# A two-direction gated delta rule: 64-wide block matrices, and the next tile pair's preparation inside the recurrence

## What is computed

```python
CHUNK = 64
gc = cumsum(chunks(g))                                   # running decay in a chunk
decay = exp(where(lower, gc[..., :, None] - gc[..., None, :], -inf))   # 64 x 64
nil = where(strict, -einsum('nbhid,nbhjd->nbhij', kb, kc) * decay, 0)  # 64 x 64
tinv = eye(64) + nil; power = nil
for _ in range(5):
    power = power @ power
    tinv = tinv + tinv @ power
w_v  = tinv @ (vc * bc)
k_cd = tinv @ (kb * exp(gc))
# the recurrence, chunk after chunk
v_new = w_v - k_cd @ state
o     = (qc * exp(gc)) @ state + (qc kc^T * decay) @ v_new
state = state * exp(g_last) + k_dec^T @ v_new
```

## Time and profile before

| | |
|---|---|
| median of 3 executions | 3482.56 us (3478.14 to 3482.67) |
| the profiled execution | 3480.33 us |
| its span, first to last instruction | 3478.5 us |
| PE busy | 3211.5 us, 92% of the span |
| DVE, ACT, POOL busy | 1343.4, 1095.5, 1170.1 us |
| mean granted clock of PE | 0.969 |
| delta stage, layer 0 | 264.0 to 635.4 us |
| delta stage, layer 1 | 2194.1 to 2496.6 us |

### The profile page before, as it was taken

How to read it: one execution, slowest core, us unless ns; L and a number is a source line. 1 busy time by engine, 2 the same in 40 slices (tenths; PEclk the granted TensorE clock), 3 DMA queues, 4 the chain that set the end, 5 groups by cost and what they waited for, 6 DMA issues and landing times.

```text
span 3478.5 us, 49823 instructions
## 1 busy us (share of the span) xinstructions
PE 3211.5 (92%) x21019; PEld 2728.1 (78%) x21019; DVE 1343.4 (39%) x1765; ACT 1095.5 (31%) x1742; POOL 1170.1 (34%) x753
## 2 busy tenths in 40 slices
PE   5998999998889999799999989899999999989997
PEld 3887888876668888588888767789877778768885
DVE  4684434234561112422222368644424631232222
ACT  2442222223552212222222244432323542232222
POOL 4234333421203333323223232544531324444443
PEclk7999999999999999899999979999999999989999
DMA  5214433210002232122222121000111013423331
GB/s 196 67 33 155 158 111 104 67 53 20 9 6 64 64 100 67 34 65 61 67 61 61 55 73 43 25 1 1 49 55 31 10 51 99 136 62 97 97 93 59
DMA packets 303660, 231.41 MB, mean 67 GB/s; under 512 B 16784, under 2 KB 275280, under 8 KB 302544
## 3 DMA queue, kind: packets, MB, share of 16 engines
q1 hardware_dynamic: 297360, 204.55, 19.7%
q0 software_dynamic: 3776, 17.91, 1.4%
q10 hardware_dynamic: 2304, 5.77, 0.4%
HBM read 217.19 MB, written 11.98 MB: 66 GB/s over the span
## 4 chain that ended last, share of the span: by engine, by line
PE 82%; DVE 8%; issue 4%; ACT 3%; POOL 2%; DMA 0%; ACTq 0%; POOLq 0%; DVEq 0%
PE ps L409 19%; PE ps L410 19%; PE ps L411 19%; PE ps L653 3%; PE ps L668 3%; PE ps L494 2%; DVE stat L1188 2%; PE ps L515 1%; PE ps L713 1%; PE ps L700 1%; PE ps L532 1%; PE ps L421 1%; PE ps L717 1%; PE ps L701 1%; DVE R L1161 1%
## 5 line engine op out<-in xcount | busy, mean ns | idle before, releaser
L1536 POOL TENSOR_TENSOR wl<-wring,wh 128x1024 fp32r<-128x1024 f32 (+1 forms) x312 | 721.1, 2314 | 1368.2 <-ACT wh L922 1368.2
L409 PE MATMUL ps<-hh,wh 128*128 128x512 f32 (+1 forms) x2592 | 932.8, 360 | 90.1 <-DVE hl L1167 77.5
L410 PE MATMUL ps<-hl,wh 128*128 128x512 f32 (+1 forms) x2592 | 915.2, 353 | 0.0
L411 PE MATMUL ps<-hh,wl 128*128 128x512 f32 (+1 forms) x2592 | 914.4, 353 | 0.0
L409 PEld LDWEIGHTS ps<-hh,wh 128*128 128x128 f32 x2592 | 497.4, 192 | 179.1 <-issue 53.8
L410 PEld LDWEIGHTS ps<-hl,wh 128*128 128x128 f32 x2592 | 498.2, 192 | 67.8 <-issue 4.1
L411 PEld LDWEIGHTS ps<-hh,wl 128*128 128x128 f32 x2592 | 497.1, 192 | 66.3
L922 ACT ACTIVATE wh<-wring 128x1024 fp32r<-128x1024 f32 (+1 forms) x312 | 307.8, 988 | 523.6 <-PE ps L411 497.4
L1471 DVE SCALAR_TENSOR_TENSOR R<-ps,modcs,R 128x512 f32<-128x512 f32 x216 | 136.3, 659 | 387.7 <-PE ps L411 386.7
L410 PE MATMUL ps<-fl,wh 128*128 128x512 f32 (+1 forms) x768 | 274.8, 358 | 0.0
L411 PE MATMUL ps<-fh,wl 128*128 128x512 f32 (+1 forms) x768 | 274.5, 357 | 0.0
(11 more groups left out here) (232 smaller groups left out, 4791.2 us busy)
## 6 DMA issues: line engine op xcount, KB each, us to landing
wring<-in_w_ffn SPq DMA_DIRECT2D x128, 512.0 KB, 4.0
wring<-in_w_in SPq DMA_DIRECT2D x116, 512.0 KB, 3.8
wboth<-in_w_mod SPq DMA_DIRECT2D x80, 512.0 KB, 6.1
wring<-in_w_branch SPq DMA_DIRECT2D x48, 256.0 KB, 2.8
wring<-in_w_out SPq DMA_DIRECT2D x16, 512.0 KB, 3.8
x_store<-R POOLq DMA_DIRECT2D x2, 3072.0 KB, 9.6
R<-x_store POOLq DMA_DIRECT2D x2, 3072.0 KB, 11.6
R<-in_w_mod SPq DMA_DIRECT2D x7, 512.0 KB, 13.4
```

The source lines that it names most:

```text
L409: mm(ps[:, t0:t1], ahk, rh[:, k, t0:t1], start=(k == 0), stop=False)
L410: mm(ps[:, t0:t1], ahk, rl[:, k, t0:t1], start=False, stop=False)
L411: last = mm(ps[:, t0:t1], alk, rh[:, k, t0:t1], start=False, stop=(k == kn - 1))
L1536: G.tensor_tensor(slot_view(wl, n % NSPL, l, name, i), w, slot_view(wh, n % NSPL, l, name, i).bitcast(F32), ALU.subtract)\
```

## The change

The block-diagonal matrices are now kept as what they are: 64 wide, one chunk in partitions 0 to 63 and the other in 64 to 127 of a [128, 4, 64] buffer. Masks and identity are 64 wide too. Then:

- Every product of two such matrices is two products of 64 x 64 x 64 per head, one for each chunk, in alternation (`halves`): chunk 0 in rows and columns 0 to 63 of the array, chunk 1 in rows and columns 64 to 127. Key and query products (`key_products`) are 64 columns wide, chunk 0 and chunk 1 in alternation.
- The transpose of the next power is no longer a transpose of ACT's copy: it is a product of its own (the transposed power squared), issued with `pw` (`halves(ps[:, 512:768], src, srcT)`). AT is a product with the identity.
- ACT's, DVE's and POOL's operations on these matrices have 256 columns instead of 512.
- `vn` and the output products compute only the chunk's 64 rows, with the two directions (which are at different chunks, `chunk = (c, 1 - c)`) in alternation, head by head; `so` alternates the directions too, and both directions' `so` come before the outputs. DVE adds both states before it adds outputs, and PE's next `vn` waits for `read_first`, that is for the state alone; with output, `so` has a mark of its own (`pe_done "S"`) for it.
- The next pass's preparation moves into the recurrence of this one: `delta_decays` (bc, W, and the exponentials for the queries, which now have two buffers) after `vn` of the first chunk, `delta_keys` (G, A) after `vn` of the second, `delta_turned` (AT) after the second chunk's products. Only `Q` and X0 stay at the head of a pass. For pass 0 the three stand ahead of the loop, and no pass's R waits for `z_saved` now.
- kcd writes its two chunks to two banks; kbe and kd share a buffer (`kbuf`).

The diff, cut to its core (ACT's and DVE's lists follow the same pattern; POOL's order is shown further down):

```diff
+        qdbuf = [[r(U0 + 5120 * d + 512 * b, 2, 4, HALF) for d in range(2)] for b in range(2)]
+        kbuf, vnbuf, vbbuf = ([r(U0 + 5120 * d + at, 4, P) for d in range(2)] for at in (1024, 2048, 4608))
+        cdbuf = [r(U0 + 5120 * d + 1536, 2, 4, HALF) for d in range(2)]
+        rbuf, wbuf, pbuf, p2buf, tbuf, t2buf, xbuf, aqbuf = (
+            [r(U0 + 5120 * d + at, 4, HALF) for d in range(2)] for at in range(2560, 4608, 256))
...
+            def halves(out, left, right):
+                for h in range(C_H):
+                    for lo in (0, HALF):
+                        last = mm(out[lo:lo + HALF, h * HALF:h * HALF + HALF], left[lo:lo + HALF, h, :],
+                                  right[lo:lo + HALF, h, :], start=True, stop=True)
+                return last
+            def delta_decays(l, s, d):
+                pe.wait_ge(*pool_done.at("R", l, s, d))
+                ps = take(pe, "bc", l, s, d)
+                rows = [flat(rbuf[d])[lo:lo + HALF, :] for lo in (0, HALF)]
+                for c, lo in enumerate((0, HALF)):
+                    mm(ps[:, 512 * c:512 * c + 256], ones[lo:lo + HALF, :], rows[c], start=True, stop=True)
+                for c, lo in enumerate((0, HALF)):
+                    last = mm(ps[lo:lo + HALF, 256:512], ones[lo:lo + HALF, 0:HALF], rows[c], start=True, stop=True)
...
                         for d in range(2):
                             src, srcT, dst, dstT = power(d, i)
                             pe.wait_ge(*(read("pw", l, s, d, i - 1) if i else read("AT", l, s, d)))
                             ps = take(pe, "pw", l, s, d, i)
-                            for h in range(C_H):
-                                last = mm(ps[:, h * P:h * P + P], srcT[:, h, :], src[:, h, :], start=True, stop=True)
+                            last = halves(ps, srcT, src)
+                            if i < 4:
+                                last = halves(ps[:, 512:768], src, srcT)
                             last.then_inc(*filled("pw", l, s, d, i))
                         for d in range(2):
                             src, srcT, dst, dstT = power(d, i)
-                            if i < 4:
-                                pe.wait_ge(*read_first("pw", l, s, d, i))
-                                for h in range(C_H):
-                                    last = tr(pair("pw", l, s, d, i)[:, 512 + h * P:512 + h * P + P], dst[:, h, :], ident)
...
+                            pe.wait_ge(*read("pw", l, s, d, i))
                             pe.wait_ge(*(read("X", l, s, d, i - 1) if i else dve_done.at("X0", l, s, d)))
+                            halves(take(pe, "X", l, s, d, i), dst, xbuf[d]).then_inc(*filled("X", l, s, d, i))
...
+                        new = [take(pe, "vn", l, n, d) for d in range(2)]
+                        for h in range(C_H):
+                            o = [new[d][at[d]:at[d] + HALF, h * P:h * P + P] for d in range(2)]
+                            for d in range(2):
+                                mm(o[d], cdbuf[d][:, chunk[d], h, :], S[:, 4 * d + h, :], start=True, stop=False)
+                            for d in range(2):
+                                ins = mm(o[d], xbuf[d][at[d]:at[d] + HALF, h, :], vbbuf[d][at[d]:at[d] + HALF, h, :],
+                                         start=False, stop=True)
...
+                        if s + 1 < TT:
+                            for d in range(2):
+                                (delta_decays, delta_keys)[c](l, s + 1, d)
                         for d in range(2):
                             pe.wait_ge(*read("vn", l, n, d))
                             pe.wait_ge(*pool_done.at("kd", l, s, d))
...
+                    if s + 1 < TT:
+                        for d in range(2):
+                            delta_turned(l, s + 1, d)
```

DVE's list in a doubling step keeps its order, for each direction first the copy of the transposed power, then the addition of X:

```diff
                         for d in range(2):
                             if i < 4:
-                                dve.wait_ge(*pe_done.at("pwT", l, s, d, i))
-                                V.tensor_copy(flat(power(d, i)[3]), pair("pw", l, s, d, i)[:, 512:1024])\
+                                dve.wait_ge(*full("pw", l, s, d, i))
+                                V.tensor_copy(flat(power(d, i)[3]), pair("pw", l, s, d, i)[:, 512:768])\
                                     .then_inc(*free("pw", l, s, d, i, by=1))
                             dve.wait_ge(*full("X", l, s, d, i))
-                            V.tensor_tensor(flat(xbuf[d]), pair("X", l, s, d, i)[:, 0:512], flat(xbuf[d]), ALU.add)\
+                            V.tensor_tensor(flat(xbuf[d]), pair("X", l, s, d, i)[:, 0:256], flat(xbuf[d]), ALU.add)\
```

More of the change, by code:

```diff
@@ L222, in power @@
         def power(d, i):
-            one, two = (pbuf[d], tbuf[d]), (p2buf[d], rbuf[d])
+            one, two = (pbuf[d], tbuf[d]), (p2buf[d], t2buf[d])
             return (*one, *two) if i % 2 == 0 else (*two, *one)
@@ L1007, in _ @@
+                for d in range(2):
+                    delta_decays(l, 0, d)
+                for d in range(2):
+                    delta_turned(l, 0, d)
                 for s in range(TT):
                     for d in range(2):
-                        act.wait_ge(*full("bc", l, s, d))
-                        if s:
-                            act.wait_ge(*full("vn", l, 2 * s - 1, d))
-                        A(flat(ebuf[d]), pair("bc", l, s, d)[:, 0:512], ACT.Exp).then_inc(*free("bc", l, s, d, by=1))
@@ L1021, in _ @@
-                    for d in range(2):
-                        act.wait_ge(*full("AT", l, s, d))
-                        A(flat(tbuf[d]), pair("AT", l, s, d)[:, 0:512], ACT.Copy).then_inc(*free("AT", l, s, d))
+                        delta_queries(l, s, d)
                     for i in range(5):
@@ new lines, in _ @@
+                        for d in range(2):
+                            t, cc = tiles[d][s], (c if d == 0 else 1 - c)
+                            if out_wanted:
+                                lo = 64 * cc
+                                o, new = Otok[lo:lo + 64, t, :], pair("so", l, n, d)[lo:lo + 64, 512:1024]
+                                dve.wait_ge(*full("so", l, n, d))
+                                if (t, cc) in seen:
+                                    V.tensor_tensor(o, new, o, ALU.add).then_inc(*free("so", l, n, d, by=1))
+                                else:
+                                    V.tensor_copy(o, new).then_inc(*free("so", l, n, d, by=1))
+                                seen.add((t, cc))
```

336 lines of the change are left out of this document (188 added, 148 removed).

## The result

The changed kernel takes **3416.68 us** (median of 4 runs, 3411.79 to 3422.39), where the kernel before took 3482.61 (4 runs, 3478.14 to 3483.76) on the same chip: a ratio of 0.9817, with a 95% interval of 0.9805 to 0.9828. It is faster, by 66 us, and inside the range of the prediction. But the forecast was 132 us, and of these only half came. The profiled execution has a span of 3417.9 us at a mean granted clock of 0.952 (before: 3478.5 and 0.969).

A forecast was written before the change was run, and what follows sets the result against it. PE, busy 92% of the span, was taken to bound the kernel. Savings of 69.0 us in layer 0 and 63.0 in layer 1, 132 together off 3480.3, gave 3350 us; own range 3300 to 3385, stated range 3300 to 3430.

The forecast's parts named there:

- the clock falls: Rival: PE's waits in doubling steps drop the clock to the 1.2 GHz level; 3395 us, or 3438; chance 0.20.
- record of the 64 x 64 pair: PE's time per matmul record in alternating 64-wide products: 0.0275 us, bounds 0.0275 and 0.055.
- doubling step, wait in it: One doubling step takes 3.8 us instead of 4.46, with PE waiting 1.15 us for DVE's copy.
- kcd to `vn`: From kcd's start to `vn`: 32 records in 1.76 us, then ACT's copies, 2.65 us in all.
- change of tile shape: Each switch of PE between full-row and 64-row tiles costs 0.15 us, bounds 0 and 0.19.
- pass without, with output: Layer 1 passes: 36.2 us without output against 45.25 before, 40.5 with output against 52.4.
- last kcd to projection: In a layer's last pass, from kcd to the first projection: 19.65 us, including 1.5 us waits for `vn` copies.
- waits for modulation weights: SP's weight loads for layer 0's modulation blocks: costed at nothing, up to 10 us if their cover fails.
- earlier start, layer 0: At layer 0's start the chain W, A, AT, Q in half-size operations becomes 3.2 us shorter.
- The overlap of the two diagonal tiles: The two chunks' 64 x 64 tiles run side by side on PE; the no-overlap rival gave 3490 us, chance 0.12.
- DVE's T(1) behind add(0): In each doubling step DVE's second transposed copy follows its first addition, so PE waits 1.15 us before X(1).
- granted clock of 1.00: PE stays at the 2.4 GHz level in the delta stages' passes, as in the profile before; no loss summed.

The follow-up runs named there:

- e6: Changed kernel with e4's unread products, modulation blocks spread evenly over layer 0's doubling steps, and last-pass ACT query work after both `vn` copies: 3380.77 us.
- e1: Changed kernel with the 64 x 64 products reordered, all four heads of chunk 0 first, then all four of chunk 1: 3464.23 us.
- e2: Changed kernel with DVE copying both directions' transposed powers before it adds to either X: 3377.85 us.
- e3: Changed kernel with all full-row matmuls first, then all 64-row ones, in `vn` and outputs, `start` and `stop` only at first and last head: 3344.91 us.
- e4: Changed kernel with unread products put into PE's waits, in doubling steps, between kcd and `vn`, and ahead of some `so`: 3381.32 us.
- e9: Changed kernel with unread products only in the first four doubling steps of each pass, 48 in all: 3415.93 us.
- e10: Changed kernel with only one unread product in each pass, between kcd and `vn`, 12 in all: 3395.55 us.
- e5: Changed kernel with decays, key products and turned matrix back at the head of their own pass, products still 64 wide: 3490.04 us.

## Why the prediction was right or wrong

Right in sign and in range; the forecast itself missed half. The outcome lies where the rival "the clock falls" put it (3395, at most 3438; chance 0.20), but that is in part luck: the clock took 35 us, and another 34 that this rival didn't have came on top. And the range held because it had been drawn to take in the clock's case; its own range for the forecast ended at 3385.

| Term of the prediction | said | measured |
|---|---|---|
| record of the 64 x 64 pair | 0.0275 us | 0.0292 |
| doubling step, wait in it | 3.8, 1.15 | 3.94, 0.93 |
| kcd to `vn` | 2.65 | 3.0 to 3.1 |
| change of tile shape | 0.15 | 0.15 |
| `vn` and output product | 2.95 | 2.94 |
| decays; `so` | 2.4; 1.1 | 2.42; 1.1 |
| pass without, with output | 36.2, 40.5 | 37.2, 41.5 |
| last kcd to projection | 19.65 | 32.2 and 28.3 (20.2 in each in e6) |
| waits for modulation weights | 0, at most 10 | 6.3 |
| earlier start, layer 0 | 3.2 | 0.6 |
| clock | 1.00 | 0.88 and 0.94 |

**What held.** The overlap of the two diagonal tiles, on which the sign hung: 0.0292 us a record in alternation, 0.058 within one tile (e1). The Trainium skill (TensorEngine Tiling (Array Packing), Restrictions and Gotchas) has the rule that different row tiles cannot access the same PSUM bank at the same time; for two tiles in different rows and different columns, writing into one bank, the measurement differs from it, and the measurement decides. What is late next in a step, DVE's T(1) behind add(0), held too (e2). So did the price of a change of shape as time on PE, 0.15 (e3).

**The step that failed** is the one that carried's "granted clock of 1.00" over to passes in which PE waits and changes its tiles all the time. It was held apart as a rival; it belonged into the sum. It cost 35 us (e4). And its mechanism in the rival was wrong: I put it into the waits of the doubling steps, "with half of the array in use", and in e9 products in these waits alone gave no time back. It falls around kcd and `vn` (e10), and the changes of shape are a part of it (e3).

**Terms that were mis-sized.** Each of twelve passes is 1.0 us longer than worked out, from the steps (4 x 0.14) and from kcd to `vn` (0.4): 12 us. The last passes: ACT's weight rounding between the two copies of `vn`, which I had not read in ACT's list, 1.04 us a chunk, some 5 in both layers. The waits in front of the modulation blocks' products, costed at nothing: 6. The start of layer 0: from the last projection to the first `pw` it was 20.6 us and is 20.0, with PE waiting 10.98 of them for the first A. The chain to A came hardly earlier for its shorter operations: nearly 3 us. With the clock's 35 this is 61 of the 69 us by which the stages missed; the other 8, in the passes with modulation blocks, I did not trace.

**The structure of the argument.** I summed two halves of a change and did not ask what each is worth alone. e5 answers: the narrow products without the moves 0.25% slower than before, the moves 73 us on top. Narrow work shortens PE's list but not the copies of `vn` and the chain to A, and a PE that waits for them ran more of its time at the 1.2 GHz level (239 us against 126). The moves pay twice, by the waits and by the clock.

## What to carry to other kernels

When an edit halves an engine's work, price the clock as a term of the sum: take the passes as they will be, with their waits and changes of tile shape, and find rows at that density before you write 1.00. Group matmuls by tile shape, full rows first and then half rows, over all heads of a product, not shape by shape within a head: here that one reordering was worth 72 us, the whole change 66. Read every engine's list at the place where two parallel chains will now end together; what stood between them under the cover of their distance comes onto the path.

## What was not expected of the hardware

- **Frequent changes of tile shape go with a lower clock.** Alternating full-row and 64-row matmuls every four records: 126 us at 1.2 GHz in the stages; the same matmuls in two groups: 37.5 us, with the same waits left in (e3).
- **Short waits are not alike.** Unread products in 48 waits of 0.93 us in the doubling steps left the clock where it was (0.950 to 0.959 in the whole kernel, 0.952 to 0.955 without); in 12 of 1.0 to 1.1 between kcd and `vn` they raised it to 0.958 to 0.961 and saved 21 us (e9, e10).
- **PE runs ahead across tiles.** With the matmuls of a tile in a block, the next block's first one starts 0.17 us before the last one of the block ahead, so that 96 records stand 0.038 apart, not 0.058 (e1).
- **Unread matmuls can pay.** With 4462 matmul records instead of 4387 in layer 1's stage, and likewise in layer 0, the kernel is 35 us faster (e4).
